# Product by product: when the Winograd quads of an MLP open, and in which order the ff parts of a chunk are made

## The reference, cut to what matters

```python
def squared_relu_mlp(h, w1, w2):
    return jnp.square(jax.nn.relu(h @ w1)) @ w2
...
    h = rms_norm(x, g[2])
    x = x + rms_norm(squared_relu_mlp(h, mlp_w1[i], mlp_w2[i]), g[3])
```

## Time and profile before

| | |
|---|---|
| median of 3 runs | 1809.09 us (1808.79 to 1809.18) |
| the profiled execution | 1806.52 us, its span 1804.7 us |
| mean granted TensorE clock | 0.983 |
| TensorE matmuls, busy | 1732.5 us (96% of the span) |
| VectorE, ScalarE, GpSimd, busy | 1070.5, 776.6, 953.9 us (59%, 43%, 53%) |

### The profile page before, as it was taken

The page is one execution under the profiler, slowest core; times in us unless marked ns, Lnnn a source line. Parts: engine busy times, 40 slices in busy tenths (PEclk is TensorE's granted clock), DMA queues, the critical chain, the costliest instruction groups (busy, mean ns, idle before and its releaser), DMA issues.

```text
span 1804.7 us, 25901 instructions
## 1 busy us (share of the span) xinstructions
PE 1732.5 (96%) x9327; PEld 1491.6 (83%) x9327; DVE 1070.5 (59%) x1715; ACT 776.6 (43%) x1301; POOL 953.9 (53%) x583
## 2 busy tenths in 40 slices
PE   8999997999999998999889999999999999999999
PEld 6888885979797887878788989788979888888887
DVE  6558557666666679856675757657848154444200
ACT  6338454343434456544434343437348432222221
POOL 3457545454545668756545454566435644444442
PEclk9999998999999999999989999999999999999999
DMA  5531112323232312122122223222210222322332
GB/s 189 126 99 54 47 59 82 107 82 116 72 117 70 106 47 98 66 82 94 59 99 89 106 82 112 76 102 86 84 60 2 93 94 93 103 94 93 105 105 70
DMA packets 46103, 158.84 MB, mean 88 GB/s; under 512 B 5744, under 2 KB 6000, under 8 KB 46000
## 3 DMA queue, kind: packets, MB, share of 16 engines
q1 hardware_dynamic: 46000, 157.45, 26.0%
HBM read 153.10 MB, written 2.10 MB: 86 GB/s over the span
## 4 chain that ended last, share of the span: by engine, by line
PE 81%; DVE 9%; ACT 4%; issue 3%; POOL 2%; DMA 1%; SPq 0%; DVEq 0%; ACTq 0%; POOLq 0%
PE PS L2171 23%; PE PS L2173 23%; PE PS L2172 23%; DVE PS L1441 2%; PE PS L2240 2%; PE PS L2276 1%; PE PS L2271 1%; PE PS L2272 1%; DVE sqb L1433 1%; DVE PS L1433 1%; DVE tmp L1433 1%; PE PS L2433 1%; DVE TL L1433 1%; DMA raw<-weights 1%; DVE wl L1433 1%
## 5 line engine op out<-in xcount | busy, mean ns | idle before, releaser
L2172 PE MATMUL PS<-XLR,wh 128*128 128x512 f32 x1216 | 474.3, 390 | 0.0
L623 POOL TENSOR_TENSOR wl<-raw,wh 128x1024 fp32r<-128x1024 f32 x109 | 262.5, 2416 | 187.8 <-ACT wh L880 186.6
L633 POOL TENSOR_TENSOR wl<-raw,wh 128x1024 fp32r<-128x1024 f32 x92 | 223.4, 2431 | 261.5 <-ACT wh L1412 120.9
L2171 PE MATMUL PS<-XHR,wh 128*128 128x512 f32 x888 | 348.9, 393 | 8.0 <-POOL wl L768 5.8
L2173 PE MATMUL PS<-XHR,wl 128*128 128x512 f32 x888 | 346.5, 390 | 0.0
L880 ACT ACTIVATE wh<-raw 128x1024 fp32r<-128x1024 f32 x171 | 179.6, 1056 | 301.1 <-PE PS L2173 255.6
L2171 PE MATMUL PS<-TH,wh 128*128 128x256 f32 (+1 forms) x872 | 257.1, 295 | 41.2 <-DVE TL L1433 23.7
L2172 PEld LDWEIGHTS PS<-XLR,wh 128*128 128x128 f32 x1216 | 229.0, 188 | 46.8
L2172 PE MATMUL PS<-TL,wh 128*128 128x256 f32 (+1 forms) x872 | 256.0, 294 | 0.0
L2173 PE MATMUL PS<-TH,wl 128*128 128x256 f32 (+1 forms) x872 | 255.9, 293 | 0.0
L685 POOL TENSOR_TENSOR wl<-raw,wh 128x512 fp32r<-128x512 f32 x90 | 122.9, 1367 | 206.6 <-DVE PS L1433 126.8
(11 more groups left out here) (370 smaller groups left out, 3376.6 us busy)
## 6 DMA issues: line engine op xcount, KB each, us to landing
raw<-weights SPq DMA_DIRECT2D x287, 512.0 KB, 3.3
X<-x_t SPq DMA_DIRECT2D x8, 256.0 KB, 6.4
out_t<-X SPq DMA_DIRECT2D x8, 256.0 KB, 4.2
KH<-rope_h SPq DMA_DIRECT2D x4, 128.0 KB, 5.1
KL<-rope_l SPq DMA_DIRECT2D x4, 128.0 KB, 5.2
QH<-XHR SPq DMA_DIRECT2D x16, 32.0 KB, 2.0
QL<-XLR SPq DMA_DIRECT2D x16, 32.0 KB, 2.0
pos_i<-positions SPq DMA_DIRECT2D x1, 256.0 KB, 9.1
```

Source lines behind the costliest of these rows:

```text
L623: pool.tensor_tensor(wl[:, WPOS[n]], raw[:, n % RING], wh[:, WPOS[n]].bitcast(F32), ALU.subtract).then_inc(w_lo, 1)
L633: pool.tensor_tensor(wl[:, s], raw[:, j], wh[:, s].bitcast(F32), ALU.subtract).then_inc(w_lo, 1)
L2171: pe.matmul(out, wa, xa, start=start, stop=False)
L2172: pe.matmul(out, wa, xb, start=False, stop=False)
```

## The change

Four things change, in both layers.

TensorE: the two waits ahead of `down_quads` go, as does the one of the last chunk. Instead each of the four first products of a phase's first pair waits, for each k, for the count of `hid` or `sums_lo` that its own operand needs.

VectorE: in chunk 0, for the tiles 0 to 5, `hidden` of the odd tile comes ahead of `even_low` of the even one. In the last chunk `odd_low` comes ahead of `quad_low` S2 and `quad_sum` S3 at tile 7.

GpSimd: the low part of A22 of a phase's first pair is made after the sums' low parts of the last ff pair. In the last chunk one whole block, for the closing down tile, is made ahead of two `add_output`.

ScalarE: the tap copies stand in the chunks 1 and 2 instead of 0 and 1; in the last chunk the block for the closing down tile is rounded ahead of `square_m(3)`.

```diff
@@ GpSimd, mlp_lows @@
                         if n >= n0 - RING:
-                            quad_lows(n0, 0, ((A11,), (A12,), (A22,), ())[n - n0 + RING])
+                            quad_lows(n0, 0, ((A11,), (A12,), (), ())[n - n0 + RING])
                         else:
                             lo_range(n + RING, n + RING + 1)
                         if t % 2:
                             sums_low(layer, 4 * c + t // 2)
+                        if t == CHUNK - 1:
+                            quad_lows(n0, 0, (A22,))
...
                 for u in range(1, quads):
                     quad_lows(n0, u)
+                    if u == quads - 1:
+                        lo_range(n0 + 2 * quads, n0 + 2 * quads + 1)
                     add_output(job, 2 * u - 1)
                     add_output(job, 2 * u)
-                lo_range(n0 + 2 * quads, after + 1)
+                lo_range(n0 + 2 * quads + 1, after + 1)
@@ ScalarE, mlp @@
-                        if layer == 0 and c < 2 and t == 3:
+                        if layer == 0 and c in (1, 2) and t == 3:
                             sc.wait_ge(dw_low_done, 1)
-                            low_taps(c)
+                            low_taps(c - 1)
...
-                square_m(3)
                 n = n0 + 2 * quads
                 hi(n)
+                square_m(3)
                 square_m(4)
@@ VectorE, mlp @@
-                        hidden(c, t)
+                        ahead = c == 0 and t < CHUNK - 2
+                        if not (ahead and t % 2):
+                            hidden(c, t)
+                        if ahead and t % 2 == 0:
+                            hidden(c, t + 1)
...
                             odd_sums(c, t)
+                            if last:
+                                odd_low(c, t)
                             if t == CHUNK - 1:
                                 quad_low(n0, 0, S2)
                                 quad_sum(n0, 0, S3)
-                            odd_low(c, t)
+                            if not last:
+                                odd_low(c, t)
@@ TensorE, product and mlp @@
                         slot, p = 4 * (at_half % 2) + k, (4 * c + k) % H_RING
+                        if u == 0:
+                            done = 2 * (pairs_done + 4 * c + k)
+                            if i in (A11, A12):
+                                pe.wait_ge(hid, done + (A11, A12).index(i) + 1)
+                            elif i in (S1, S2):
+                                pe.wait_ge(sums_lo, done + (S1, S2).index(i) + 1)
...
                     up_tile(c, 0)
-                    pe.wait_ge(hid, 2 * (pairs_done + 4 * c))
-                    pe.wait_ge(sums_lo, 2 * (pairs_done + 4 * c))
                     down_quads(c - 1)
...
-                pe.wait_ge(sums_lo, 2 * (pairs_done + 4 * NCHUNK))
                 down_quads(NCHUNK - 1)
```

## The result

The changed kernel takes 1768.26 us, median of 4 runs (1764.75 to 1769.49), against 1808.94 us of the kernel before (4 runs, 1807.5 to 1809.18). The ratio is 0.9774, 95% interval 0.9757 to 0.9791: 40.7 us faster. The forecast was 1755 us, so some 13 us of the expected gain did not come. The profiled execution took 1768.53 us where the working gave 1752.3: 16.2 us are to be accounted for.

The account below looks back on a forecast made before the run. TensorE, 96% busy, bounds the kernel; only its idle or low-clock time can be won: 45.0 idle + 14.2 clock - 5.0 staying = 54.2 us off 1806.5, so 1752.3, plus 2.6 for the median: 1755 us. Range 1748 to 1771.

Parts of the forecast that it names:

- the case that I held likeliest: Whole kernel: the time comes as forecast, 1750 to 1762 us; chance 0.70.
- rival 2: All eight openings start in time but the clock still falls at each; 14.2 us stay, 1769 us; chance 0.10.
- rival 3: VectorE bounds the quads; some 2 us wait at the second pair's third product in each of eight phases, 1771; chance 0.10.
- my own signs: New profile: no MLP TensorE wait over 2.5 us, clock 1.00 up to layer 0's norm; wrong if M waits in every phase.
- What stays in chunk 0, 2.4 us: Each layer's chunk 0 keeps 1.0 us waiting at S1 and 1.4 us at the second pair's third product.
- 7.2 us earlier: Chunk 0: VectorE's odd low part gains 1.5, 1.2, 3.0 and 1.5 us over pairs 0 to 3, 7.2 in all.
- 1.5 more in pair 3: Chunk 0, last pair of tiles: VectorE's idle is filled by late work, bringing the odd low part 1.5 us earlier.
- the 1.23 us of the earlier trace: Chunk 0: duration of a sum with both operands in SBUF, against 0.7 us for others; basis for the 2.4 us.
- The clock, 14.2 us: Eight low-clock stretches behind the openings, 28.5 us at half clock, lose 14.2 us; all of it was taken as won back.
- left it high: Stretch 144 to 148: a 1.2 to 1.3 us wait kept clock 1.00, so remaining waits that size should too.
- Room of 0.4 us: Chunks 1 and 2: VectorE's reads have 0.4 us to spare before the product needing them, so no wait there.
- The 0.80, 0.47, 2.35 and 1.09 us: Chunk 3 waits: 0.80 and its smaller layer 1 like go but for about 0.1; 2.35 and closing tile's 1.09 go.

Follow-up runs that it names:

- kept busy: Changed kernel with 20 extra identity matmuls in each chunk 0 between A11 and S1, filling TensorE's wait; 1767.32 us.
- the fastest kernel: S1 early plus three edits: fifth read ahead of S4's low part, second bank opened only ahead of S2, chunk 3's last A11 ahead of two square sums; 1760.49 us.
- S1 early: Changed kernel with VectorE's tile 7 operations ahead of tile 6's low part, S1's low part and S4 sum later, ScalarE rounding tile 6 before S2; 1767.06 us.
- the sum cut: Changed kernel with the first pair's S1 sum in both chunks 0 covering 4 of 512 columns; 1764.67 us.
- the order alone: Changed kernel with TensorE's old waits put back, keeping the other engines' new order; 1781.17 us.
- the closing block back: Closing block of chunk 3 at its old place on ScalarE and GpSimd: on the changed kernel 1766.58 us; on the fastest kernel with VectorE's queue changed again 1767.02.

## Why the prediction was right, and where it was short

The mechanism was in the main as forecast. Both waits ahead of a phase went, in all eight phases; the openings of the chunks 1 and 2 have no wait at all, and their clock stays up; 128 added waits cost nothing that a row shows, and the quads run at 0.12 us a matmul as before. Nothing became slower. But the case that I held likeliest, 1750 to 1762, did not come. The time, 1768.3, lies in the range only because the range took in the rivals 2 and 3, and its closeness to their 1769 and 1771 is chance: the clock stayed low at two openings and not at eight, and the reads cost 0.7 us a phase and not 2. By my own signs the waits on M in every phase speak against my sum for VectorE.

**What stays in chunk 0, 2.4 us, is the term that was most too small:** it is 5.6 us (18.63 - 15.4 + 2.4). I let VectorE's odd low part come 7.2 us earlier; it came at 307.51 against 309.48 in the kernel before, less the 3.0 us by which this execution runs later, so 4.9 us earlier. By pairs of tiles the gains were 1.4, 1.2, 2.3 and 0.0 us, where I had 1.5, 1.2, 3.0 and 1.5. The 2.3 us that lack are two things, seen in VectorE's and ScalarE's timelines of the changed kernel:

```profile
302.28 0.69 DVE L1437 TENSOR_TENSOR TL<-PS,TH 128x512 fp32r<-128x512 f32 x1 [1.70 <-ACT tmp L1166]
...
300.68 0.60 ACT L1154 ACTIVATE wh<-PS 128x512 fp32r<-128x512 f32 x1 [2.25 <-DVE PS L1437]
```

First, "1.5 more in pair 3 (its idle is filled by work that was late)": it is not. VectorE still idles 1.70 us, for ScalarE, whose queue is held by the S2 weight, which waits for VectorE's own S4 sum. This wait moves with VectorE, so lateness can't fill it. Second, the S1 sum took 1.60 us in place of about 0.8, since it now starts while an instruction of GpSimd runs that ends only at 293.77; I had noted that such a sum can be slow (the 1.23 us of the earlier trace rows), and put it in the bounds but at another place. The two make 2.3 of the 3.2 us; the rest is not traced.

**The clock, 14.2 us.** The sum was right on the chunks 1 to 3 (six stretches, 10.2 us). In the chunks 0 the clock still fell, as rival 2 had it for all openings, because S1's wait was 2.84 us and not 1.0. But the run with TensorE kept busy shows that this cost nothing there, since VectorE was late by as much. The 1.2 to 1.3 us of idle that "left it high" were one execution's: in two of the fourteen the clock falls behind the same idle, see the end.

**The reads.** Room of 0.4 us in the chunks 1 and 2 was a lack of 0.5: rival 3's mechanism, in every phase, at a third of its price (0.7 us in place of 2). In the chunks 0 to 2 its place was as said, the third product of the second pair. There, in the chunks 1 and 2, it is cured by two moves of a few lines, as the fastest kernel shows.

**Chunk 3.** The 0.80, 0.47, 2.35 and 1.09 us all went. The 0.77 us on GpSimd's A11 of the last pair, which stands behind two sums of squares, had no wait before it in the kernel before (GpSimd had it at about 601.6, TensorE came for it at 602.28), and I had not looked for what is queued there.

**The median.** I added 2.6 us to the profiled time because of how the two stood before. After, both are the same (1768.53 and 1768.26), perhaps because the start of the profiled execution before was short, see the end.

## What to carry to other kernels

When a wait is removed, walk the queue of the engine that was waited for, and its helpers' queues, to the next place where it is needed: part of what TensorE gained at the head of a phase came back where VectorE's queue set the end. A wait that two engines have on each other (here ScalarE's on VectorE's sum, and VectorE's on ScalarE's copy) was not filled by being late: it was 1.70 us before and after, and moved along. Before pricing a low clock, ask whether the engine would only arrive earlier at its next wait: filling the idle kept the clock at 1.00 and won nothing.

## What the runs showed of the hardware

- **An elementwise sum waits for GpSimd's whole instruction.** VectorE's sum of two SBUF operands takes 0.70 us with GpSimd idle. If it starts well inside an instruction of GpSimd, it ends 0.55 us behind that instruction's end: in the changed kernel GpSimd ends at 293.77 and the sum, started at 292.72, at 294.32. With 4 columns in place of 512 it still took 1.07 us. The Trainium skill, "SBUF — State Buffer", section "SBUF: two separate sides", says that the two engines share a pair of ports as an exclusive lock, held for a whole instruction by the one that starts first, and that the other is fully blocked; the traces agree. An operation of VectorE with one operand in SBUF and one in PSUM, such as the low parts, kept its 0.69 us beside GpSimd. It is a matter of which starts first: the S1 sums of the third and fourth pair in the chunks 0 to 2 took 0.69 us in the kernel before, where GpSimd's instruction began 0.05 us behind them, and take 1.42 to 1.45 us in the changed one, where it is already running. These twelve sums make some 9 us, about what VectorE's busy time grew by (1070.5 to 1079.7 us) without a new instruction.
- **Which idles the clock fell behind.** At the openings and closing tiles: behind 2.35, 2.70, 2.71, 2.84 to 2.87, 3.12, 3.13 and 3.69 us of idle there was a low stretch each time; behind 1.10, 1.60 and 1.82 never; 2.49 and 2.47 us (S1 early) had none; of two waits of 2.31 us (the sum cut) and of two of 1.81 us (the order alone) one had it and the other not. At 144 to 148 us all fourteen executions have one and the same idle of 1.31 to 1.35 us: behind it the clock stays up in twelve and is low for 6.8 us in two (S1 early, from 149.0, and kept busy, from 147.9). So the length of the idle alone does not decide it. Filling 2.34 of the 2.84 us with matmuls on the identity took it away, in both layers.

```profile
149.10:155.80 6.70, 6.46 (x20) 4.88 (x19) 3.69 (x11) 4.18 (x11) 4.14 (x5) 0.50 0.37 108
```

- **The start varies.** Nine of the fourteen profiled executions have a low stretch of 3.4 or 6.8 us that begins between 9.3 and 11.5 us, though all kernels run the same instructions there. In four (S1 early, the sum cut and the two with the closing block back) the view gives no low stretch, but the clock's first record is at 15.8 to 15.9 us, and matmuls of 512 columns come every 0.43 us up to there (14.92 and 15.35 in S1 early) against 0.23 in the kernel before (13.26 and 13.49). The profiled execution of the kernel before is the only one that stays at the upper level from 7.5 us on. It is 3.0 us ahead of the changed kernel from 20 us on: 1.4 us because a load of x lands later in the changed kernel (ScalarE waits 1.93 us for it, 0.38 before), the rest by the clock. That is part of the scatter of 1.4 to 7.4 us between runs.
